# Gated linear recurrence: only the wanted blocks of each level, as 32x32 and 64x64 products over three banks, values two units later

## The chip, the cores and the metric

The kernel runs on one core of one Trainium2 chip. The metric is the time of an execution on the device, in microseconds; lower is better. Times come from several runs of the same program; a profile is one more execution, recorded by the hardware.

## The reference

Two transformer blocks run one after the other on 256 tokens of width 1024, each with two layers, all in float32. The change touches one mixer family of the second block, gated linear attention: four heads of GLA (keys of 32) and four heads of HGRN2 (keys of 64), values of 64.

```python
def chunked_gated_linear_attention(q, k, v, log_g):
    '''o_t = S_t^T q_t,  S_t = diag(exp(log_g_t)) S_{t-1} + k_t v_t^T, chunkwise.'''
    ...
        o_inter = jnp.einsum('bhik,bhkv->bhiv', q_ * jnp.exp(b_), state)
        rel = jnp.where(causal, b_[:, :, :, None, :] - b_[:, :, None, :, :], NEG)
        attn = jnp.einsum('bhik,bhjk,bhijk->bhij', q_, k_, jnp.exp(rel))
        o_intra = jnp.einsum('bhij,bhjv->bhiv', attn, v_)
```

Written without chunks: output token i is the sum over j <= i of (sum over the key's channels of q_i k_j exp(b_i - b_j)) v_j, where b is the running sum of the logarithm of the gate.

## The kernel before

**Levels.** The exponent b_i - b_j must not be split at a far border, or one factor overflows. The kernel therefore splits the pairs (i, j) by levels. At level l the tokens lie in blocks of 2n, n = 2^l, and a pair belongs to the level if j is in the first half of a block and i in the second. The border between the halves lies between them, so both factors are at most 1. `gaps` and `factors` build, for each level, one array GE that holds k times its decay in first halves and q times its decay in second halves. Levels 0 to 6 lie within 128 tokens; level 7 crosses from the first 128 tokens to the last 128; a product of plain k and q supplies the diagonal.

**Units.** There are 16 units in a layer: 8 heads (`FAM` has families 0, 1, 2; family 0 the GLA heads with 32 key channels, the others HGRN2 with 64) times two halves t of the tokens. Units 0 to 7 are GLA. For a unit TensorE forms eight products of 128x128 (L1706 for seven levels, L1708 for the diagonal) into PSUM banks 0 and 1, and for t = 1 the cross product of level 7 (L1711) into bank 2. Each product is a whole 128x128, of which the level wants only some blocks. VectorE multiplies the 1024 columns by a table of ones and zeros, `lvl_upper` (L1809, into `MASKED`), and adds the eight levels (L1811, into `AA`); ScalarE copies the cross product (L1748, into `ACR`). TensorE then multiplies by the values (L1685, and L1688 for the cross part) into bank 3.

**Order.** Every engine has an order written out by hand. `GLA_ORDER` lists the steps of the recurrence, `weave` puts after each of them one step of the other mixers (compressed attention, then four passes of softmax attention: NSA for t = 0 and 1, differential for t = 0 and 1). In step u TensorE issues the products of unit u, then the values of unit u-1, then its step of the others. An engine executes its instructions in that order, and waits for another engine by semaphores:

- TensorE's products of unit u wait for `gla_read` of unit u-1 (VectorE's mask has left banks 0 and 1), its values for `gla_A` and `gla_cross_out`.
- VectorE's mask waits for `gla_prod` of its unit. Its step of the other mixers stands behind its mask and sum: L1566 to L1574 (normalising the compressed key, read by TensorE's L1405), L1578 to L1587 (softmax of the compressed scores, read by L1419), L1067 to L1071 (scale, bias and maximum of a softmax), L1078 to L1081 (its sum and weights, read by L1029).
- TensorE's steps of the other mixers are L1399, L1405, L1412, L1419, L1424, and in a softmax pass L1022 (scores), L1029 (transposes) and L1038 (values); ScalarE's exponentials are L1047.
- POOL computes `gaps` and `factors` of families 1 and 2; for family 2 it waits for the products of unit 7.

In the setup POOL builds the level tables (`setup_pool`) into `lvl_upper`.

## Time and profile before

| | us |
|---|---|
| median of 3 runs | 2918.5 (2915.23 to 2920.84) |
| the profiled execution, its own time | 2915.66 |
| its span, first to last instruction | 2914.0 |
| TensorE busy (products) | 2657.3 (91%) |
| VectorE busy | 706.7 (24%) |
| ScalarE busy | 463.4 (16%) |
| POOL busy | 124.9 (4%) |

The two stretches with the recurrence are from 971 to 1113 us (layer 0 of the second block) and from 1657 to 1805 us (layer 1). Busy shares there differ from those of the whole: a share of the span says how long an engine had something under way, and not that it set the pace. A row of the time line gives the start, the time to the end of the last, the engine, the line, what is written and read, the shapes and the number of instructions merged in the row; in brackets stands how long the engine was idle before, and what ended that. A float32 product is two instructions, so 14 in a row are seven products. "32*128 32x128" is a weight block of 32 rows by 128 columns, and 128 moving columns on 32 rows. The clock in the tables (PEclk) is the share of 2.4 GHz that was granted: 0.50 is 1.2 GHz.

### The profile page before, as it was taken

The numbers are of one execution on the slowest core, as the hardware profiler recorded it, in microseconds if no ns is written. First come the engines' busy times: TensorE is split into PE (matmuls) and PEld (weight loads), VectorE is DVE, ScalarE is ACT, GpSimd is POOL, SyncE is SP. The second block draws the span as 40 slices with busy tenths as digits, with TensorE's granted clock in tenths as the row PEclk, the third lists the DMA queues.
The fourth block names the chain that finished last, engine by engine and source line by source line (L and its number), as shares of the span: only waits on it lengthen the run. The fifth ranks groups of instructions, "written<-read, shape, count | busy, mean of one in ns | idle before, by whom it ended". The sixth has DMA issues, their size and how long they took to land. (4 is left out here: it accounts for less than half of the span.)

```text
span 2914.0 us, 43737 instructions
## 1 busy us (share of the span) xinstructions
PE 2657.3 (91%) x19755; PEld 1489.0 (51%) x19755; DVE 706.7 (24%) x1244; ACT 463.4 (16%) x754; POOL 124.9 (4%) x320
## 2 busy tenths in 40 slices
PE   8899999999988776999979776799999999999997
PEld 7566558566534663444434475435445344353443
DVE  3434523434421653000011455200001000010002
ACT  1522311412212221001011321100000000000001
POOL 3011000010000110000000020000000000000000
PEclk9999999999999557999999755799999999999998
DMA  7321333312335101344434300399999999999990
GB/s 224 117 73 59 126 110 132 129 59 87 116 123 139 58 1 58 116 149 139 155 122 124 110 1 1 114 366 358 388 350 370 374 361 381 357 370 376 355 367 26
DMA packets 181230, 542.06 MB, mean 186 GB/s; under 512 B 26896, under 2 KB 38320, under 8 KB 181040
## 3 DMA queue, kind: packets, MB, share of 16 engines
q1 hardware_dynamic: 167744, 536.95, 51.1%
q10 hardware_dynamic: 12992, 1.22, 0.4%
q8 instruction: 158, 2.59, 0.3%
q0 software_dynamic: 304, 1.05, 0.1%
q14 instruction: 32, 0.26, 0.0%
HBM read 538.12 MB, written 1.05 MB: 185 GB/s over the span
## 5 line engine op out<-in xcount | busy, mean ns | idle before, releaser
L367 PE MATMUL psum<-ring,hT 128*128 128x512 f32 (+2 forms) x1856 | 783.0, 580 | 14.8 <-ACT area L606 13.2
L367 PEld LDWEIGHTS psum<-ring,hT 128*128 128x128 f32 x1856 | 346.0, 194 | 414.8 <-issue 393.5
L2106 PE MATMUL psum<-ring,area 128*32 128x448 f32 x4608 | 439.2, 539 | 2.6 <-ACT area L2208 2.0
L2106 PEld LDWEIGHTS psum<-ring,area 128*32 128x32 f32 x4608 | 150.0, 110 | 285.5 <-issue 282.0
L493 PE MATMUL psum<-hT,ring 128*128 128x256 f32 x768 | 166.5, 379 | 0.0
L493 PEld LDWEIGHTS psum<-hT,ring 128*128 128x128 f32 x768 | 145.8, 190 | 20.6 <-issue 1.0
L2125 PE MATMUL psum<-area 128*32 128x256 f32 x2688 | 149.8, 380 | 2.0 <-ACT area L2226 2.0
L2125 PE MATMUL psum<-ring,area 128*32 128x256 f32 x2688 | 151.5, 380 | 0.0
L2106 PE MATMUL psum<-area 128*32 128x448 f32 x1536 | 147.3, 539 | 0.0
L2125 PEld LDWEIGHTS psum<-area 128*32 128x32 f32 x2688 | 85.7, 110 | 60.2 <-ACT area L2226 3.9
L2259 DVE TENSOR_TENSOR area<-area,psum 128x1344 f32<-128x1344 f32 x16 | 24.9, 1554 | 372.1 <-PE psum L2106 372.1
L1706 PE MATMUL psum<-area 32*128 32x128 f32 (+1 forms) x448 | 103.2, 416 | 12.5 <-DVE area L1655 10.3
L2125 PEld LDWEIGHTS psum<-ring,area 128*32 128x32 f32 x2688 | 84.9, 110 | 57.0 <-issue 2.7
L1706 PEld LDWEIGHTS psum<-area 32*128 32x128 f32 (+1 forms) x448 | 94.2, 315 | 20.6 <-DVE area L1655 10.5
L1863 PE MATMUL psum<-ring,area 128*128 128x512 f32 x224 | 98.1, 601 | 1.2 <-ACT area L1874 1.2
L2106 PEld LDWEIGHTS psum<-area 128*32 128x32 f32 x1536 | 50.6, 110 | 93.8 <-issue 93.8
L2226 ACT ACTIVATE area<-psum 128x384 f32<-128x384 f32 x56 | 24.9, 488 | 408.5 <-PE psum L2121 408.5
L418 PE MATMUL psum<-ident,xn 128*128 128x128 f32 x132 | 30.1, 419 | 61.8 <-DVE xn L444 61.8
L1863 PEld LDWEIGHTS psum<-ring,area 128*128 128x128 f32 x224 | 43.1, 193 | 55.6 <-issue 54.2
L1029 PE MATMUL psum<-ident,area 128*128 128x128 f32 x120 | 23.5, 366 | 52.5 <-DVE area L1081 30.5
L2250 DVE TENSOR_TENSOR x<-x,psum 128x1024 f32<-128x1024 f32 x16 | 19.5, 1222 | 201.4 <-PE psum L2089 201.4
L2495 POOL DMA_DIRECT2D area<-in_p_dram x2 | 1.5, 758 | 1515.7 <-DVEq L214 1515.7
(453 smaller groups left out, 2426.8 us busy)
## 6 DMA issues: line engine op xcount, KB each, us to landing
ring<-in_w_in_dram SPq DMA_DIRECT2D x96, 1024.0 KB, 5.0
ring<-in_moe_w_gate_dram SPq DMA_DIRECT2D x96, 896.0 KB, 6.7
ring<-in_moe_w_up_dram SPq DMA_DIRECT2D x96, 896.0 KB, 7.8
area<-in_moe_w_down_dram SPq DMA_DIRECT2D x112, 512.0 KB, 7.5
ring<-in_moe_w_down_dram SPq DMA_DIRECT2D x112, 512.0 KB, 7.0
area<-in_moe_w_gate_dram SPq DMA_DIRECT2D x32, 896.0 KB, 6.7
area<-in_moe_w_up_dram SPq DMA_DIRECT2D x32, 896.0 KB, 8.3
ring<-in_w_out_dram SPq DMA_DIRECT2D x16, 1024.0 KB, 5.0
```

The costliest lines, as they stand in the source:

```text
L367: last = nc.tensor.matmul(acc(g)[:, t, 0:d["n"]], lhs(kk, t), w[:, k, :], start=kk == 0, stop=kk == d["nk"] - 1)
L418: last = nc.tensor.transpose(PS[0:m, bank0 + b // 2, (b % 2) * S + t * P:(b % 2) * S + (t + 1) * P], src, IDENT)
L493: last = nc.tensor.matmul(acc(g)[:, j // 2, (j % 2) * S:(j % 2) * S + S], half_view(n, (4, 512))[:, k % 4, j * P:(j + 1) * P], HT[:, k, :] ...
L1029: last = nc.tensor.transpose(PS[:, 4 + h // 2, ((h % 2) * T + j) * P:((h % 2) * T + j + 1) * P], SCORES[:, h, j * P:(j + 1) * P], IDENT)
L1706: nc.tensor.matmul(PS[:, l // 4, (l % 4) * P:(l % 4 + 1) * P], GE[f % 2][r, l, tok], GE[f % 2][r, l, tok], start=True, stop=True)
L1863: last = nc.tensor.matmul(PS[:, 2 * t + dh, :], HFT[:, 2 * i + k, t * P:(t + 1) * P], w[:, k, 512 * dh:512 * dh + 512], start=i + k == 0, ...
L2106: last = nc.tensor.matmul(PS[32 * j:32 * j + 32, 3 * p + b, 0:PIECE], XG[:, k, 32 * b:32 * b + 32], expert_slot(j0 + j // 2, GROUP * (j % ...
L2125: return nc.tensor.matmul(PS[32 * jj:32 * jj + 32, b, 0:256], HET[:, i // 4, b, 32 * (i % 4):32 * (i % 4) + 32], ring_cols(chunk_place(i) ...
L2226: nc.scalar.activation(HET[:, c], PS[:, 6 + c % 2, 0:BLOCKS * P].rearrange("p (b s) -> p b s", b=BLOCKS), ACT.Copy).then_inc(ms("HT"), 1)
L2250: nc.vector.tensor_tensor(X[:, t, :], X[:, t, :], banks(6, 2), ALU.add).then_inc(ms("added"), 1)
L2259: nc.vector.tensor_tensor(h, h, PS[:, 3 * p:3 * p + 3, 0:PIECE], ALU.mult).then_inc(ms("h"), 1)
L2495: pool.dma_start(PP, A["p_2"][L].rearrange("b (t p) c -> p (b t) c", p=P))\
```

## The change

Each level now forms only the blocks that it wants. Levels 0 to 4 and the diagonal have their pairs within 32 tokens: four blocks of 32x32 each, written to the partitions of their own tokens, so that six levels lie side by side in 192 columns. Level 5 is two blocks of 32x32, level 6 one of 64x64, level 7 stays a 128x128. Units go over banks 0, 1 and 2 in turn instead of sharing 0 and 1. VectorE masks and adds 192 columns instead of 1024. ScalarE copies the rest of each unit (levels 5, 6 and, for t = 1, 7: 96 or 224 columns) without a mask, after VectorE has read the bank. The values are five products and, for t = 1, a sixth, and follow two units later; three sets of `PARTS` hold a unit's factors. PSUM columns and parts that no product writes are set to zero once in a layer by VectorE. ScalarE's copy of the first eight outputs moves from unit 8 to unit 10.

```diff
-        MASKED = view(20656, 8 * P)
-        AA = [view(6456 + 128 * i, P) for i in range(2)]
-        ACR = [view(6712 + 128 * i, P) for i in range(2)]
+        MASKED = [view(20656 + 192 * i, 192) for i in range(2)]
+        PARTS = [view(a, 288) for a in (6456, 21040, 21328)]
...
             def out(u):
+                a = PARTS[u % 3]
                 pe.wait_ge(sem("gla_A"), 16 * L + u + 1)
+                pe.wait_ge(sem("gla_far"), 16 * L + u + 1)
...
-                last = nc.tensor.matmul(dst, AA[u % 2], U2[:, t, v0:v0 + HD], start=True, stop=t == 0)
+                for b in range(4):
+                    r = slice(32 * b, 32 * b + 32)
+                    nc.tensor.matmul(dst[r], a[r, 0:32], U2[r, t, v0:v0 + HD], start=True, stop=False)
+                last = nc.tensor.matmul(dst, a[:, 32:160], U2[:, t, v0:v0 + HD], start=False, stop=t == 0)
                 if t == 1:
-                    pe.wait_ge(sem("gla_cross_out"), 8 * L + u // 2 + 1)
-                    last = nc.tensor.matmul(dst, ACR[u // 2 % 2], U2[:, 0, v0:v0 + HD], start=False, stop=True)
+                    last = nc.tensor.matmul(dst, a[:, 160:288], U2[:, 0, v0:v0 + HD], start=False, stop=True)
...
-                if u:
-                    pe.wait_ge(sem("gla_read"), 16 * L + u)
-                for l in range(LEVELS):
-                    nc.tensor.matmul(PS[:, l // 4, (l % 4) * P:(l % 4 + 1) * P], GE[f % 2][r, l, tok],
-                                     GE[f % 2][r, l, tok], start=True, stop=True)
-                last = nc.tensor.matmul(PS[:, 1, 3 * P:4 * P], TT[r, FAM[f][1], tok], TT[r, FAM[f][0], tok],
-                                        start=True, stop=True)
+                if u >= 3:
+                    pe.wait_ge(sem("gla_far"), 16 * L + u - 2)
+                ps = PS[:, u % 3]
+                for b in range(4):
+                    blk, c = slice(t * P + 32 * b, t * P + 32 * b + 32), slice(32 * b, 32 * b + 32)
+                    for l in range(5):
+                        nc.tensor.matmul(ps[c, 32 * l:32 * l + 32], GE[f % 2][r, l, blk], GE[f % 2][r, l, blk],
+                                         start=True, stop=True)
+                    nc.tensor.matmul(ps[c, 160:192], TT[r, FAM[f][1], blk], TT[r, FAM[f][0], blk], start=True, stop=True)
+                    if b % 2 == 0:
+                        up = slice(t * P + 32 * b + 32, t * P + 32 * b + 64)
+                        nc.tensor.matmul(ps[c, 192 + 32 * b:224 + 32 * b], GE[f % 2][r, 5, blk], GE[f % 2][r, 5, up], start=True, stop=True)
+                last = nc.tensor.matmul(ps[0:64, 224:288], GE[f % 2][r, 6, t * P:t * P + 64],
+                                        GE[f % 2][r, 6, t * P + 64:t * P + 128], start=True, stop=True)
...
-                if u:
-                    out(u - 1)
+                if u >= 2:
+                    out(u - 2)
                 yield
+            out(14)
             out(15)
...
+                    s.eng.wait_ge(sem("gla_read"), 16 * L + u + 1)
+                    if u >= 3:
+                        s.eng.wait_ge(sem("gla_out"), 16 * L + u - 2)
+                    n = 96 + 128 * UNITS[u][2]
+                    s.after(nc.scalar.activation(PARTS[u % 3][:, 64:64 + n], PS[:, u % 3, 192:192 + n], ACT.Copy)
+                            .then_inc(sem("gla_far"), 1), "gla_far")
...
+            s.do(nc.vector.memset(PS[:, 0:3, 192:288], 0.0))
+            for a in PARTS:
+                s.do(nc.vector.memset(a[:, 32:64], 0.0))
...
-                    s.after(nc.vector.tensor_tensor(MASKED, banks(0, 2), mt_t[:, :], ALU.mult)
+                    s.after(nc.vector.tensor_tensor(MASKED[u % 2], PS[:, u % 3, 0:192], near_t[:, :], ALU.mult)
                             .then_inc(sem("gla_read"), 1), "gla_read")
-                    s.after(nc.vector.tensor_reduce(AA[u % 2], MASKED.rearrange("p (l c) -> p c l", l=8), AX.X, ALU.add).then_inc(sem("gla_A"), 1), "gla_A")
+                    if u >= 3:
+                        s.eng.wait_ge(sem("gla_out"), 16 * L + u - 2)
+                    s.after(nc.vector.tensor_reduce(PARTS[u % 3][:, 0:32], MASKED[u % 2].rearrange("p (l c) -> p c l", l=6),
+                                                    AX.X, ALU.add).then_inc(sem("gla_A"), 1), "gla_A")
...
-            s.do(g.tensor_copy(MT[:, LEVELS, :], IDENT))
+            for b in range(4):
+                r = slice(32 * b, 32 * b + 32)
+                s.do(g.tensor_copy(NEAR[r, 0:5, :], MT[r, 0:5, r]))
+                s.do(g.tensor_copy(NEAR[r, 5, :], IDENT[r, r]))
```

In the changed kernel the products are lines 1712 (levels 0 to 4), 1714 (diagonal), 1717 (level 5), 1718 (level 6) and 1721 (level 7), the values 1688 (four of 32x64), 1689 and 1691, VectorE's mask and sum 1821 and 1825, ScalarE's copy 1763.

TensorE's order from the transposed compressed key (L1405) to the compressed scores (L1412), with unit 3 between them, before:

```order
L1405 MATMUL psum<-ident,area 128x128
L1706 MATMUL psum<-area 128x128 x7
L1708 MATMUL psum<-area 128x128
L1711 MATMUL psum<-area 128x128
L1685 MATMUL psum<-area 128x64
L1412 MATMUL psum<-area 128x32 x8
```

and after (here a row's number counts products, each of two passes):

```order
L1405 MATMUL psum<-ident,area 128x128
L1712 MATMUL psum<-area 32x32 x5
L1714 MATMUL psum<-area 32x32
L1717 MATMUL psum<-area 32x32
...
L1718 MATMUL psum<-area 64x64
L1721 MATMUL psum<-area 128x128
L1688 MATMUL psum<-area 32x64 x4
L1689 MATMUL psum<-area 128x64
L1691 MATMUL psum<-area 128x64
L1412 MATMUL psum<-area 128x32 x8
```

Left out are the same rows for the other three blocks of 32 tokens (L1717 for every second one). Nine products of unit 3 have become 28, and the values in that step are those of unit 1 instead of unit 2.

VectorE and ScalarE, the step of unit 2, with what each instruction waits for; before, VectorE:

```order
L1809 TENSOR_TENSOR area<-psum,lvl_upper 128x1024 [waits gla_out,gla_prod,cmp_by_vector]
L1811 TENSOR_REDUCE area<-area 128x128 [waits gla_read]
L1569 RECIPROCAL small<-small 128x1 [waits cmp_by_scalar,gla_A]
L1570 SCALAR_TENSOR_TENSOR area<-psum,small,param_rows 128x64 [waits dve_steps]
L1571 COPY area<-area 128x64 [waits dve_steps]
```

after, VectorE:

```order
L1821 TENSOR_TENSOR area<-psum,lvl_upper 128x192 [waits gla_prod,cmp_by_vector]
L1825 TENSOR_REDUCE area<-area 128x32 [waits gla_read]
L1569 RECIPROCAL small<-small 128x1 [waits cmp_by_scalar,gla_A]
L1570 SCALAR_TENSOR_TENSOR area<-psum,small,param_rows 128x64 [waits dve_steps]
L1571 COPY area<-area 128x64 [waits dve_steps]
```

and ScalarE after, where before there was a copy (L1748) only for units with t = 1:

```order
L1763 ACTIVATE area<-psum 128x224 [waits gla_read,cmp_by_scalar]
L1467 ACT_TABLE_LOAD [waits cmp_by_vector]
L1467 ACTIVATE small<-small 128x1 [waits gla_far]
L1763 ACTIVATE area<-psum 128x96 [waits gla_read,cmp_by_scalar]
L1470 ACTIVATE area<-psum 128x128 [waits cmp_by_tensor,gla_far]
```

Nothing has changed its place between the steps; the unit's work on VectorE is narrower, and ScalarE has a copy in every unit, which waits for VectorE's mask.

## Rows read from the trace of the kernel before

**Rows 1.** Stretches: us, busy us and count of each engine, clock, DMA.

```profile
972.00:1113.00 141.00, 105.20 (x508) 94.68 (x508) 80.74 (x79) 30.96 (x91) 21.52 (x48) 0.55 0.00 1
1657.00:1805.00 148.00, 115.11 (x507) 104.07 (x507) 81.13 (x81) 30.72 (x91) 21.69 (x48) 0.50 0.00 0
1062.00:1076.00 14.00, 11.61 (x105) 10.81 (x104) 10.72 (x11) 1.24 (x2) 5.18 (x12) 0.99 0.00 1
663.00:669.00 6.00, 6.00 (x119) 5.94 (x117) 1.47 (x6) 0.77 (x2) 0.53 (x2) 0.50 0.02 6
```

**Rows 2.** Time line of TensorE's products, layer 1, units 2 to 4.

```profile
1668.38 3.32 PE L1706 MATMUL psum<-area 32*128 32x128 f32 x14 [0.86 <-DVE area L1809]
...
1676.18 0.48 PE L1405 MATMUL psum<-ident,area 128*128 128x128 f32 x1 [3.01 <-DVE area L1571]
1676.58 3.35 PE L1706 MATMUL psum<-area 32*128 32x128 f32 x14
1679.73 0.63 PE L1708 MATMUL psum<-area 32*128 32x128 f32 x2
1680.16 0.63 PE L1711 MATMUL psum<-area 32*128 32x128 f32 x2
1680.72 0.69 PE L1685 MATMUL psum<-area 128*128 128x64 f32 x2
...
1692.07 0.69 PE L1419 MATMUL psum<-ident,area 128*128 128x128 f32 x2 [4.04 <-DVE area L1587]
```

**Rows 3.** The same, units 10 to 15.

```profile
1751.03 7.04 PE L1038 MATMUL psum<-area 128*128 128x64 f32 x32
...
1762.75 1.26 PE L1022 MATMUL psum<-area 32*128 32x128 f32 x16
...
1774.11 1.12 PE L1029 MATMUL psum<-ident,area 128*128 128x128 f32 x4 [5.35 <-DVE area L1081]
...
1801.88 1.97 PE L1029 MATMUL psum<-ident,area 128*128 128x128 f32 x8 [8.64 <-DVE area L1081]
```

**Rows 4.** Time line of VectorE, layer 1, units 2 to 4.

```profile
1672.22 1.23 DVE L1809 TENSOR_TENSOR area<-psum,lvl_upper 128x1024 f32<-128x1024 f32 x1 [1.84 <-PE psum L1708]
1673.48 1.90 DVE L1811 TENSOR_REDUCE area<-area 128x128 f32<-128x1024 f32 x1
...
1675.93 0.19 DVE L1571 COPY area<-area 128x64 f32<-128x64 f32 x1
...
1684.81 0.42 DVE L1580 TENSOR_REDUCE small<-area 128x8 f32<-128x256 f32 x1
...
1688.34 1.94 DVE L1811 TENSOR_REDUCE area<-area 128x128 f32<-128x1024 f32 x1
1690.31 0.42 DVE L1584 TENSOR_REDUCE small<-area 128x8 f32<-128x256 f32 x1
```

**Rows 5.** The same, unit 11.

```profile
1763.56 1.93 DVE L1811 TENSOR_REDUCE area<-area 128x128 f32<-128x1024 f32 x1
1765.52 1.22 DVE L1067 SCALAR_TENSOR_TENSOR area<-psum,causal_bias 128x1024 f32<-128x1024 f32 x1
```

**Rows 6.** Time line of TensorE, first block, 64x64 weights at the lower clock.

```profile
666.50 1.04 PE L803 MATMUL psum<-area 64*64 64x32 f32 x16
667.36 1.04 PE L799 MATMUL psum<-area 64*64 64x32 f32 x16
```

**Rows 7.** The page's costliest groups: us busy, ns of one.

```profile
L2125 PE MATMUL psum<-area 128*32 128x256 f32 x2688 | 149.8, 380 | 2.0 <-ACT area L2226 2.0
```

**Rows 8.** Time line of TensorE, layer 1, scores of the first softmax pass.

```profile
1704.01 3.09 PE L1022 MATMUL psum<-area 64*128 64x128 f32 x16
1707.03 3.35 PE L1706 MATMUL psum<-area 32*128 32x128 f32 x14
```

**Rows 9.** Groups of instructions by shape, 1657 to 1806 us, ScalarE.

```profile
L1748 ACT ACTIVATE area<-psum 128x128 f32<-128x128 f32 x8 | 2.2, 277 | 35.8 <-PE psum L1711 35.7
```

**Rows 10.** Time line of TensorE, layer 0, unit 0.

```profile
971.51 3.35 PE L1706 MATMUL psum<-area 32*128 32x128 f32 x14 [5.17 <-DVE area L1655]
```

More of the change, by code:

```diff
@@ L126, in blocks_kernel @@
         IDENT2 = eye_t[:, :]
-        mt_t = sb("lvl_upper", (LEVELS + 1) * P)
-        MT = mt_t[:, :].rearrange("p (l c) -> p l c", l=LEVELS + 1)
+        near_t = sb("lvl_upper_32", 6 * 32)
+        NEAR = near_t[:, :].rearrange("p (l c) -> p l c", l=6)
         cb_t = sb("causal_bias", T * S)
@@ L1702, in gla_pe @@
                     pe.wait_ge(sem("hg_GE"), 2 * L + f)
-                if u:
-                    pe.wait_ge(sem("gla_read"), 16 * L + u)
-                for l in range(LEVELS):
-                    nc.tensor.matmul(PS[:, l // 4, (l % 4) * P:(l % 4 + 1) * P], GE[f % 2][r, l, tok],
-                                     GE[f % 2][r, l, tok], start=True, stop=True)
-                last = nc.tensor.matmul(PS[:, 1, 3 * P:4 * P], TT[r, FAM[f][1], tok], TT[r, FAM[f][0], tok],
-                                        start=True, stop=True)
+                if u >= 3:
[12 more added lines that the diff above has]
+                                        GE[f % 2][r, 6, t * P + 64:t * P + 128], start=True, stop=True)
                 if t == 1:
-                    last = nc.tensor.matmul(PS[:, 2, (u // 2 % 2) * P:(u // 2 % 2 + 1) * P], GE[f % 2][r, 7, 0:P],
-                                            GE[f % 2][r, 7, P:S], start=True, stop=True)
+                    last = nc.tensor.matmul(ps[:, 288:416], GE[f % 2][r, 7, 0:P], GE[f % 2][r, 7, P:S],
+                                            start=True, stop=True)
                 last.then_inc(sem("gla_prod"), 1)
-                if u:
-                    out(u - 1)
+                if u >= 2:
+                    out(u - 2)
                 yield
+            out(14)
             out(15)
@@ L1743, in gla_act @@
                 elif kind == "unit":
-                    if UNITS[u][2] == 1:
-                        s.eng.wait_ge(sem("gla_prod"), 16 * L + u + 1)
-                        if u >= 4:
-                            s.eng.wait_ge(sem("gla_out"), 16 * L + u - 3)
-                        s.after(nc.scalar.activation(ACR[u // 2 % 2], PS[:, 2, (u // 2 % 2) * P:(u // 2 % 2 + 1) * P],
-                                                     ACT.Copy).then_inc(sem("gla_cross_out"), 1), "gla_cross_out")
-                    if u == 8:
+                    if u == 10:
                         s.eng.wait_ge(sem("gla_out"), 16 * L + 8)
@@ L2366, in setup_pool @@
             wide_low = view(1024, P)
+            MT = view(1152, LEVELS * P).rearrange("p (l c) -> p l c", l=LEVELS)
             for l in range(LEVELS):
```

4 lines of the change are left out of this document (1 added, 3 removed).

## The prediction

> **What bounds the kernel now.** I began with the granted clock and the busy shares of the two stretches in which the gated recurrence runs [rows 1]. One stands in each layer of the second block, 141 us long in layer 0 and 148 us in layer 1. TensorE is busy 105 of 141 and 115 of 148 us, VectorE 81 in both, and no weights arrive. The clock is at its lower level (1.2 GHz) in all of layer 1's stretch; in layer 0's, 14 us ran near 2.4 GHz, and that stretch is about 7 us shorter. The stage is a relay between TensorE, VectorE and ScalarE with TensorE the runner on most legs, so its own order of time comes next [rows 2, 3], then VectorE's [rows 4, 5]. The reader is to see two sorts of TensorE time: work back to back, and waits that end with VectorE. Four such waits have VectorE's work on a unit in front of what TensorE wants.
>
> - The products of unit 2 wait 0.86 us until unit 1 has been read from the same two banks [rows 2].
> - L1405 waits 3.01 us for the copy L1571, which stands behind unit 2's mask and sum (1.23 + 1.90 us) [rows 2, 4].
> - L1419 waits 4.04 us for a chain whose first link, L1584, starts the moment unit 4's sum (1.94 us) ends [rows 2, 4].
> - L1029 waits 5.35 us in the differential attention. There L1067 starts as unit 11's sum ends, although its scores (L1022, 1.26 us from 1762.75) are there at about 1764.1 [rows 3, 5].
>
> The wait of 8.64 us [rows 3] is a softmax of 2048 columns on VectorE and ScalarE; the change takes at most 0.1 us from it.
>
> **VectorE's work on a unit.** L1067 takes 1.22 us for 1024 columns, L1580 0.42 for 256, so a column costs 1.04 ns and an instruction 0.15 us besides [rows 4, 5]. The mask on 192 columns then takes 0.36. The strided sum is dearer, 1.93 us for 1024 columns [rows 5]; its share for 192 is 0.36, and with an instruction's fixed part counted again 0.5; I take 0.45. A unit goes from 3.15 us (with gaps) to 0.85: 2.3 us less, 32 times. That is 74 us of VectorE, and nearly all of it hidden. What shows, for layer 1: 0.9 (now three banks) + 2.3 (L1405) + 2.3 (L1419, whose exponentials are ready by then) + 1.4 (L1029: 1765.5 less 1764.1) + 0.1 = **7.0 us**. For layer 0 I take the same; its waits have the same causes.
>
> **TensorE's work on a unit.** Each product is two passes, and a pass is what a row counts. A pass with weights of 128 columns and 128 moving ones costs 0.43/2 = 0.215 us (L1708 to L1711), and a run of 14 takes 3.15, which is 0.14 more; from the last pass of a run to the next run in another shape of the array goes 0.56 instead of 0.43 [rows 2]. So a change of shape costs 0.14 + 0.13 = 0.27 us. L1038, with half as many moving columns (64), still costs 7.04/32 = 0.22 a pass [rows 3]: a pass costs the longer of its weight load and its product, not their sum. At the same low clock 64x64 weights run in 0.86/16 = 0.054 a pass, two tiles of the array at a time, hence 0.107 a pass in one tile [rows 1, 6]. No row has 32 columns on both sides. Half of 0.107 is 0.054; that is what the two sizes at hand (128: 0.215, 64: 0.107) extrapolate to, and it is my value. The bounds are 0.107 (no gain below 64 columns) and 0.014 (0.054 in four column tiles fully at once, as L2125 runs: 149.8/2688 = 0.056 us a pass where its 256 columns alone take 0.21 at the high clock [rows 7]).
>
> How far do the four column tiles of a unit overlap? L2125 changes tile every second pass. The new unit stays in one tile for 14, 12, 14 and 12 passes. The nearest row is L1022 with two runs of eight in two tiles: 3.02 us to the next start, less 0.27, is 12.8 passes of 0.215 for 16 [rows 8]. So a run starts some three passes before the one ahead of it ends. Three changes of tile save nine of 52 passes: 43 x 0.054 = 2.3 us.
>
> Per unit, in passes (TensorE's order is shown above):
> - removed: 16 passes, 3.44 us, and 0.27 for the shape. The cross product of every second unit (0.43) stays.
> - added: the 32x32 run 2.3 + 0.27; the 64x64 product 2 x 0.107 + 0.27 = 0.48; the four 32x64 value products, each in its own tile, 2 x 0.107 and a little, 0.27, + 0.27 = 0.54; in every second unit 0.27 more, because the 128x128 cross product is now a shape of its own.
> - even unit: 2.57 + 0.48 + 0.54 = 3.59 against 3.71, so 0.12 less; odd unit: 0.15 more. The mean is nothing, though the number of products has trebled.
>
> Some 12 of 16 units lie on the path (those ahead of the softmax waits don't), so +0.2 us at most. At the end of the stage values of two units instead of one are due between L1029 and L1038: +0.5. **A layer changes by -7.0 + 0.7 = -6.3 us, both together by -12.6.**
>
> **Hidden edits.** ScalarE's copy is 0.28 us for 128 columns [rows 9]; now it copies 96 or 224 of every unit, behind VectorE's mask. Its readers come two units later, so it costs nothing; if ScalarE were late by a whole step, TensorE would wait at L1688. The four memsets (0.7 us at 0.42 for 256 columns and 0.1 to 0.15 for the small ones) delay the compression's input, and TensorE stands idle for 5.17 us before unit 0, until its factors are there [rows 10]. POOL's eight small copies for one large stand in the setup, 0.3 us each or less; the first products that need these constants are far behind. Queues of DMA are not touched.
>
> **The sum.** The profiled execution took 2915.66 us (span 2914.0), the median of the runs is 2918.5. Against its own time the sum gives 2903 if layer 0 keeps its stretch at the high clock and, with 7 us more, 2910 if not. Against the median, which I take because that stretch need not come in each run, it is 2918.5 - 12.6 = 2905.9, so **2906 us**. A measurement of this kernel can tell about 0.2%, 5.8 us, from no change.
>
> **Rivals.**
> 1. *Small passes in one row group do not overlap* (slower). All 32x32 products of a unit read the same 32 or 64 partitions. If a pass there costs load plus product, 0.107, the run takes 43 to 52 x 0.107 = 4.6 to 5.6 us instead of 2.3, on 12 units of each layer: +27 to +40, less 6: 2960 to 2986. The price decides from 0.066 a pass on: there 43 x 0.012 us on 12 units is 6.2 us a layer, and gain and loss balance. For it: no row shows 32 columns. Against it: L1706 lies in one row group too, and there the load hides [rows 2, 3]. Chance 0.11; a price between would give 2925 to 2950. The Trainium skill (TensorE: Matmul & The Clock Gate, Part 3, "What overlaps and what doesn't") states just this: a weight load overlaps with products in flight only when the row group differs. By that rule L1706 would take 0.43 a pass, and the trace has 0.215, so I hold to the row.
> 2. *The long runs are serial*: a run waits for the last pass of the one before, or a 32-column pass costs 0.066. 52 x 0.054 = 2.8 us, +0.5 x 12 = +6 a layer: the gain on VectorE is paid back, 2917. For it: only two tiles were seen in L1022. Chance 0.17.
> 3. *The column tiles overlap nearly fully*, as in L2125: the run takes about 1.2 us, another 1.1 x 12 = 13 us a layer: 2880. Against it are runs of 14 instead of 2. Chance 0.10.
> 4. *The sum is right, but layer 0 loses its high clock*: smaller products, more changes of shape. It had 141 us where layer 1 had 148 [rows 1]: 2915.66 - 12.6 + 7 = 2910. Chance 0.12.
> 5. *The change does not take the waits away*, because ScalarE's copy, which waits on VectorE's mask, becomes what TensorE waits for. It would show as L1712 waiting on L1763. Its time is that of rival 2; its chance is in that one.
>
> The forecast has 0.50. The range **2890 to 2922** holds it, rivals 2 and 4 and the dearer half of 3. Faster by over 0.2% means below 2912.7: forecast 0.50, rival 3 0.10, and two thirds of rival 4, 0.08: 0.68. Within 0.2%: rival 2 and the rest of 4: 0.21. Slower: 0.11.
>
> **What would show it.** In the profile after: L1712's run from its first start to L1718's in 2.2 to 2.7 us at the low clock; L1821 near 0.36 and L1825 near 0.45 us; L1405 waiting under 1 us and L1419 under 2.3; L1029 after the last scores still 8 us or so; L1712 never waiting for L1763. Layer 1's stretch from L1712's first start to L1038's last run should be 141 to 142 us instead of 148. Wrong would be a run of 4 us or more (rival 1), 2.9 (2) or 1.2 (3), or a wait of TensorE on L1763.

## The result and the profile after

The changed kernel takes **2891.1 us** (median of 4, 2889.8 to 2892.2), the kernel before, run beside it, 2919.1 (2915.2 to 2920.8): a ratio of **0.9906, interval 0.9889 to 0.9923**. That is 28 us faster, where 13 were forecast. The direction held, and the range by 1.1 us; the size did not. The profiled execution took 2891.88 us, its span is 2890.2; it is 23.8 us shorter than that of the kernel before. The times of one kernel go with its mean granted clock: the runs of the kernel before made here go from 2923.3 us at 0.912 to 2907.3 at 0.920 (one of 6954 us left out). So of the 28 us a few can be clock.

The two stretches, in the view of [rows 1]:

```profile
972.00:1112.00 140.00, 111.71 (x1259) 96.51 (x1259) 44.92 (x83) 34.12 (x100) 21.63 (x49) 0.50 0.01 1
1648.00:1787.00 139.00, 111.70 (x1259) 96.49 (x1259) 44.18 (x80) 33.96 (x99) 21.62 (x48) 0.50 0.00 1
```

A *pass* is one of the two instructions of a float32 product. VectorE has gone from 81 to 44 us; TensorE is about as busy as it was (112 us in both, 105 and 115 before), with 1259 passes instead of 508. The clock (0.50) is low in both layers now; the 14 us near 2.4 GHz in layer 0 are gone. From here on a *stage* is the time from the first product of unit 0 to the start of the last L1038, read from the time line: 141.3 us in layer 0 and 147.9 in layer 1 before, 135.3 in both after.

TensorE's time line of layer 1, which answers to [rows 2, 3]:

```profile
1660.74 0.47 PE L1405 MATMUL psum<-ident,area 128*128 128x128 f32 x1 [0.79 <-DVE area L1571]
1661.14 0.74 PE L1712 MATMUL psum<-area 32*32 32x32 f32 x10
...
1661.70 0.26 PE L1712 MATMUL psum<-area 32*32 32x32 f32 x1
...
1662.72 0.26 PE L1712 MATMUL psum<-area 32*32 32x32 f32 x1
...
1663.49 0.47 PE L1718 MATMUL psum<-area 32*64 32x64 f32 x2
1663.89 0.79 PE L1721 MATMUL psum<-area 32*128 32x128 f32 x2
1664.61 0.44 PE L1688 MATMUL psum<-area 32*32 32x64 f32 x8
1664.98 0.69 PE L1689 MATMUL psum<-area 128*128 128x64 f32 x2
...
1674.24 0.69 PE L1419 MATMUL psum<-ident,area 128*128 128x128 f32 x2 [2.55 <-DVE area L1587]
...
1752.32 1.12 PE L1029 MATMUL psum<-ident,area 128*128 128x128 f32 x4 [5.02 <-DVE area L1081]
...
1779.13 1.97 PE L1029 MATMUL psum<-ident,area 128*128 128x128 f32 x8 [8.45 <-DVE area L1081]
```

From start to start: the 52 passes of 32x32 take 2.35 us, the 64x64 product 0.40, the four small value products 0.37. A *column tile* is the part of TensorE's array that holds 32 columns of weights; a unit's run of 32x32 products goes through four of them. Passes of one tile start every 0.0533 us. The second tile's first pass (1661.70) comes 0.56 us after the run's start, though the first tile has 14 passes, 0.75 us, and the fourth tile's (1662.72) after 1.58 us, though 40 passes, 2.13 us, lie before it. A tile so starts 3.5 passes before the one ahead of it ends. The waits at L1405 and L1419 are 0.79 and 2.55 us instead of 3.01 and 4.04. No product waits for ScalarE's copy. VectorE and ScalarE, unit 2, which answer to [rows 4]:

```profile
1659.07 0.36 DVE L1821 TENSOR_TENSOR area<-psum,lvl_upper 128x192 f32<-128x192 f32 x1 [1.69 <-PE psum L1718]
1659.46 0.48 DVE L1825 TENSOR_REDUCE area<-area 128x32 f32<-128x192 f32 x1
...
1660.49 0.20 DVE L1571 COPY area<-area 128x64 f32<-128x64 f32 x1
```

```profile
1659.52 0.25 ACT L1763 ACTIVATE area<-psum 128x96 f32<-128x96 f32 x1 [0.56 <-DVE area L1821]
```

### The profile page after: what moved, and what is told of

The parts are those of the page before. It is cut to its first block, busy times and chain, and to the rows that moved or that the text cites. A ratio compares the mean times of both kernels' runs of the same rounds, so it can differ in the third digit from the quotient of the medians.

```text
span 2890.2 us, 46780 instructions
## 1 busy us (share of the span) xinstructions
PE 2650.3 (92%) x21227; PEld 1475.8 (51%) x21227; DVE 633.8 (22%) x1252; ACT 468.9 (16%) x770; POOL 127.9 (4%) x327
## 4 chain that ended last, share of the span: by engine, by line
PE 54%; DVE 3%; ACT 2%; issue 0%; DVEq 0%; ACTq 0%; PEldq 0%
PE psum L2121 20%; PE psum L367 12%; PE psum L2140 10%; PE psum L1878 3%; PE psum L2096 1%; PE psum L2104 1%; PE psum L1261 1%; PE psum L418 1%; PE psum L1712 1%; PE psum L2136 1%; PE psum L1038 1%; ACT area L1047 0%; PE psum L1022 0%; PE psum L1029 0%; DVE area L1067 0%
## 5 line engine op out<-in xcount | busy, mean ns | idle before, releaser
L367 PE MATMUL psum<-ring,hT 128*128 128x512 f32 (+2 forms) x1856 | 780.5, 578 | 14.8 <-ACT area L606 13.2
L367 PEld LDWEIGHTS psum<-ring,hT 128*128 128x128 f32 x1856 | 345.2, 193 | 413.2 <-issue 391.8
L2140 PEld LDWEIGHTS psum<-area 128*32 128x32 f32 x2688 | 85.7, 110 | 60.2 <-ACT area L2241 3.9
L1712 PE MATMUL psum<-area 32*32 32x32 f32 (+1 forms) x1280 | 74.0, 239 | 9.0 <-DVE area L1654 9.0
L1712 PEld LDWEIGHTS psum<-area 32*32 32x32 f32 (+1 forms) x1280 | 69.7, 149 | 17.3 <-DVE area L1654 9.2
L1029 PE MATMUL psum<-ident,area 128*128 128x128 f32 x120 | 23.5, 366 | 48.7 <-DVE area L1081 26.9
L2233 ACT ACTIVATE area<-psum 128x1344 f32<-128x1344 f32 x16 | 20.5, 1291 | 269.7 <-PE psum L2121 269.7
```

The source lines that it names most:

```text
L367: last = nc.tensor.matmul(acc(g)[:, t, 0:d["n"]], lhs(kk, t), w[:, k, :], start=kk == 0, stop=kk == d["nk"] - 1)
L1712: nc.tensor.matmul(ps[c, 32 * l:32 * l + 32], GE[f % 2][r, l, blk], GE[f % 2][r, l, blk], start=True, stop=True)
L2140: return nc.tensor.matmul(PS[32 * jj:32 * jj + 32, b, 0:256], HET[:, i // 4, b, 32 * (i % 4):32 * (i % 4) + 32], ring_cols(chunk_place(i) ...
```

## The experiments

All runs are of this program on one core; ratios are to runs of the kernel before on the same chip. Columns "1405", "1029b" are the time from the first product of unit 0 to L1405 and to the L1029 of the second pass, in layer 1; up to there every kernel is at the low clock. "High" is the length of a stretch at high clock within a stage. All in us. Stages, waits and clocks are read from one profiled execution of each kernel.

| kernel | median | ratio (interval) | 1405 | 1029b | stage 0 (high) | stage 1 (high) |
|---|---|---|---|---|---|---|
| before | 2919.1 | 1 | 19.1 | 85.7 | 141.3 (13.6) | 147.9 (0) |
| after | 2891.1 | 0.991 (0.989-0.992) | 12.7 | 75.2 | 135.3 (0) | 135.3 (0) |
| e1 alternate | 2863.8 | 0.982 (0.980-0.984) | 8.9 | 64.1 | 119.8 (0) | 119.5 (3.4) |
| e2 smalls last | 2891.8 | 0.992 (0.990-0.994) | 12.7 | 75.6 | 134.2 (3.4) | 135.9 (0) |
| e3 before, narrow VectorE | 2888.9 | 0.991 (0.989-0.993) | 15.9 | 80.4 | 133.0 (13.6) | 133.2 (13.7) |
| e4 wider VectorE | 2899.4 | 0.995 (0.993-0.996) | 14.4 | 78.2 | 137.5 (3.4) | 137.8 (3.4) |
| e5 VectorE as before | 2897.7 | 0.993 (0.991-0.995) | 15.6 | 80.0 | 139.3 (3.4) | 139.3 (3.4) |
| e6 alternate, far too | 2849.1 | 0.977 (0.975-0.978) | 8.3 | 60.6 | 114.8 (3.4) | 114.8 (3.4) |
| e7 level 6 twice | 2895.0 | 0.992 (0.990-0.994) | 13.4 | 76.9 | 137.3 (3.4) | 136.7 (3.4) |
| e8 values one behind | 2883.7 | 0.989 (0.987-0.990) | 13.7 | 75.7 | 128.2 (13.6) | 134.8 (0) |
| e9 level 6 inside | 2900.7 | 0.993 (0.991-0.995) | 13.7 | 77.6 | 138.9 (0) | 138.2 (3.4) |
| e10 e1, VectorE as before | 2869.5 | 0.984 (0.982-0.985) | 12.7 | 69.2 | 123.9 (3.4) | 124.0 (3.4) |
| e11 e6, values one behind | 2845.7 | 0.974 (0.972-0.977) | 8.3 | 60.3 | 110.8 (3.4) | 110.6 (3.4) |
| e12 e6, other order | 2839.3 | 0.973 (0.971-0.975) | 8.3 | 60.5 | 107.1 (3.4) | 107.1 (3.4) |
| e13 before, narrow sum | 2896.1 | 0.994 (0.992-0.996) | 17.7 | 83.1 | 136.5 (13.7) | 136.9 (13.6) |
| e14 e5 in one bank | 2907.3 | 0.997 (0.996-0.998) | 17.0 | 81.3 | 141.3 (3.4) | 141.6 (3.4) |
| e15 e11, order 2 | 2838.8 | 0.974 (0.972-0.976) | 8.3 | 63.3 | 108.8 (3.4) | 108.3 (3.5) |
| e16 e6, order 2 | 2833.3 | 0.972 (0.971-0.974) | 8.2 | 58.3 | 106.2 (0) | 106.2 (0) |

### VectorE's part: e3, e13, e4, e5

e3 and e13 edit the kernel before, e4 and e5 the changed one:

```diff
 # e3 (e13 keeps the mask product whole); both leave columns 192 to 1023 out of the result
-nc.vector.tensor_tensor(MASKED, banks(0, 2), mt_t[:, :], ALU.mult)
+nc.vector.tensor_tensor(MASKED[:, 0:192], PS[:, 0, 0:192], mt_t[:, 0:192], ALU.mult)
-nc.vector.tensor_reduce(AA[u % 2], MASKED.rearrange("p (l c) -> p c l", l=8), ...)
+nc.vector.tensor_reduce(AA[u % 2][:, 0:32], MASKED[:, 0:192].rearrange("p (l c) -> p c l", l=6), ...)
 # e5, ahead of the mask; a second one with 146 columns ahead of the sum (e4: 58 and 96)
+s.do(nc.vector.tensor_reduce(view(6744, 82), bc(CB[:, 0, 0:82].unsqueeze(2), [P, 82, 8]), AX.X, ALU.add))
```

> The kernel before, with the mask product and the sum over levels cut from 1024 to 192 columns of 128 partitions; the other columns are left out of the result, TensorE's work is the same as before. Theory A (my prediction's VectorE part: 7.0 us of TensorE's waits a layer go, the rest of the 12.7 us that the change gained a layer is TensorE's own): a stage of about 141 us instead of 147.9 in layer 1, the kernel about 2905 us. Rival B (VectorE's shorter work is the whole gain, the small products cost what the large ones did): 135 us, about 2892 us. Rival C (TensorE was bound by itself and the waits move elsewhere): 147 us, 2918 us.

> The kernel before, with only the sum over levels cut from 1024 to 192 columns (1.92 to about 0.48 us; the other columns are left out of the result), the mask product still on 1024 columns. In the run with both cut, the stage of layer 1 shrank by 14.7 us, of which about 8 us came with a 13.7 us stretch of high clock that the kernel before has only in layer 0; anchor by anchor, where both were at the low clock, it was 5.4 us up to the first L1029. Theory A (VectorE's part at equal clock is 7 us for 2.31 us a unit, so that the sum alone, 1.44 us a unit, is 3 to 5 us): L1405 about 2 us and L1419 about 3.5 us earlier than before (17 and 31.5 us after the start), the stage 143 to 145 us if it stays at the low clock; the kernel about 2909 us, or 2902 us with a high stretch in layer 1. Rival B (VectorE's shorter work really is worth 14.7 us a layer without the clock): 139 us at the low clock.

> The changed kernel with two idle sums on VectorE in each unit (464 and 768 elements of a constant), so that the mask product ends about 1.23 us and the unit's sum about 3.15 us after the start, as in the kernel before; TensorE's work is that of the change. Theory A (a hand count of the stage with TensorE's durations from the changed kernel and VectorE's from the one before): the stage grows by about 5 us to 140.5 us, the kernel by 10 to about 2901 us. Rival B (two units of slack and three banks hide VectorE whatever it takes, the gain is all TensorE's own): 135.3 us, 2891 us. Rival C (VectorE was the whole gain): 148 us, 2916 us or more.

> The changed kernel with two larger idle sums on VectorE (656 and 1168 elements): in the last run the two took 0.64 and 0.95 us, so a unit cost VectorE 2.43 us and not the 3.15 us of the kernel before, and the stage of layer 1 grew from 135.3 to 137.8 us. With 0.88 and 1.44 us it should be as in the kernel before. Theory A (what VectorE costs a unit is partly hidden by three banks and two units of slack, the rest shows at L1405 and L1419): 139 to 141 us a stage, the kernel 2900 to 2903 us. Rival B (the added 0.72 us a unit is all on the path of 16 units): 149 us, 2920 us. Rival C (what is hidden stays hidden): 138 us, 2899 us.

e3 took 2888.9 us, what its rival B names: VectorE's columns alone seem to be worth the whole change. The granted clock forbids that reading. Windows of e3 and, at the same work, of the kernel before, layer 1:

```profile
1728.00:1742.00 14.00, 11.83 (x108) 11.07 (x107) 6.84 (x13) 3.68 (x11) 5.73 (x13) 0.99 0.00 1
```

```profile
1741.00:1755.00 14.00, 12.19 (x55) 11.63 (x56) 3.38 (x3) 5.55 (x10) 7.51 (x16) 0.50 0.00 0
```

e3 does twice the passes there. The same L1038 x32 as in [rows 3], 7.04 us, takes 3.74 in e3, and a unit's 14 passes 1.82 instead of 3.35:

```profile
1730.29 3.74 PE L1038 MATMUL psum<-area 128*128 128x64 f32 x32
1733.95 1.82 PE L1706 MATMUL psum<-area 64*128 64x128 f32 x14
...
1746.01 1.12 PE L1029 MATMUL psum<-ident,area 128*128 128x128 f32 x4 [6.18 <-DVE area L1081]
```

Two comparisons are free of the clock. Up to 1029b in layer 1, all at the low clock, e3 is 5.4 us earlier, e13 2.7. In layer 0 before, e3 and e13 have the same high stretch: stages 141.3, 136.5 and 133.0. Of both cuts' 8.2 us 3.2 are there by L1405, 2.1 come at L1419 and 2.1 at L1029 of the third pass; the other 0.8 come because the high stretch begins earlier against the work. Without these VectorE is worth **7.4 us** a layer in the old order, and the sum alone 4.4. The prediction's 7.0 stands. e13 gave less than A's 2 and 3.5 us (1.4 by L1405, 2.7 by L1419); its median of 2896 lies below the 2902 that A gave for a high stretch in layer 1, and no run shows why.

e4 undershot its own aim (2.43 us a unit instead of 3.15), and its stage grew by 2.5 us instead of 5. e5 comes near the aim (0.84 + 0.36 + 1.37 + 0.48 = 3.05 us); its groups of VectorE in layer 1:

```profile
L1826 DVE TENSOR_REDUCE area<-causal_bias 128x146 f32<-128x1168 f32 x16 | 21.9, 1370 | 0.6
L1821 DVE TENSOR_REDUCE area<-causal_bias 128x82 f32<-128x656 f32 x16 | 13.4, 836 | 36.0 <-PE psum L1721 18.1 <-PE psum L1718 17.8
```

With VectorE as slow as before, the new kernel has a stage of 139.3 us: theory A by the stage, though the median, 2897.7, lies 2 us below A's and nearer to C's. That is 4.1 us more than after, and 5.4 at equal clock (5.0 in layer 0), since 1.3 us come back between 1029b and the scores of the third pass (17.8 us against 19.1), where e5 has 3.4 us of high clock. The rest of the 12.7 us, 7.3, is TensorE's, the banks' and the lag's. 7.4 for VectorE in the old order and 7.3 for the rest are 2.0 us more than both together bring: either hides a part of the other.

### The banks: e14

```diff
-                if u >= 3:
-                    pe.wait_ge(sem("gla_far"), 16 * L + u - 2)
-                ps = PS[:, u % 3]
+                if u >= 1:
+                    pe.wait_ge(sem("gla_far"), 16 * L + u)
+                ps = PS[:, 0]
```

> The changed kernel with VectorE's work as before (stage 139.3 us, 2898 us) and with all units in bank 0 instead of taking turns over three, so that the products of a unit wait for the mask and the copy of the unit before, much as in the kernel before. Theory A (three banks hide 1 to 3 us a layer of VectorE's 3.15 us a unit, at units with no other step between): the stage 140.5 to 142.5 us, 2900 to 2905 us, and the mask of 1.2 us plus ScalarE's copy of 0.36 us shown ahead of L1712. Rival B (the values of two units ago and the other mixers' step fill that time): 139.3 us, 2898 us. Rival C (the waits show in every unit, 1 us or more): 150 us or more.

The stage grew by 2.0 and 2.3 us (A: 1 to 3), and the wait stands where A put it:

```profile
1662.51 0.71 PE L1712 MATMUL psum<-area 32*32 32x32 f32 x10 [1.93 <-ACT area L1763]
```

So the banks hide about the 2.0 us by which the two parts above overlap. e14 is the kernel nearest to the one before in everything but TensorE's products and the lag: 141.6 us, or 142.9 if the high clock gave it the same 1.3 us as e5, against 147.9. Those 5.0 us are what the prediction had as +0.7.

### The price of shapes: e7, e9, e2

```diff
 # e7: the level 6 product once more, into the same place
+                nc.tensor.matmul(ps[0:64, 224:288], GE[f % 2][r, 6, t * P:t * P + 64],
+                                 GE[f % 2][r, 6, t * P + 64:t * P + 128], start=True, stop=True)
 # e9: the same product under "if b == 2" inside the loop over b, instead of behind it
 # e2: in out(), the 128-row products first (start=True), then the four 32-row ones
```

> The changed kernel with the 64-column product of level 6 (L1718, 0.40 us from start to next start) issued twice in each unit, into the same place. This parts the price of a product into its passes and what comes once for the change of shape. Theory A (two passes of 0.107 us, and 0.19 us once): the pair takes 0.61 us, a stage 2.5 to 3 us more, the kernel about 2896 us. Rival B (each product costs its 0.40 us): the pair 0.80 us, a stage 5 us more, 2901 us.

> The changed kernel with the 64x64 product of level 6 in the middle of the 32x32 run (after the second of four column tiles) instead of behind it; the same products, but the 32x32 shape is entered twice in a unit. Theory A (entering the shape of 32 columns costs about 0.06 us, and 3 of 13 passes no longer overlap the tile before, 0.16 us): 0.2 us a unit, stage 137.5 to 138.5 us instead of 135.3, the kernel about 2896 us. Rival B (each change of shape costs 0.27 us, the price of my prediction, plus the overlap): 0.43 us a unit, stage 140 to 142 us, 2903 us. Rival C (shapes don't matter at all): 0.0 to 0.1 us a unit, 2891 to 2893 us.

> The changed kernel, with the four 32-row value products of a unit issued after its 128-row ones, directly ahead of the next unit's 32x32 run; same products. Even units then have three changes of shape instead of four, odd units three instead of five. Theory A (what is paid beside the passes is the change of shape, dearer for wider weights: about 0.12 us for one to 32 columns and 0.28 for one round through 128): 0.1 us less in even units, 0.3 in odd ones, a stage of about 133 us instead of 135.3, the kernel about 2886 us. Rival B (the price hangs on the products, not on their order): 135.3 us, 2891 us.

e7, time line, unit 2 of layer 1: two more passes put 0.21 us more between L1718 and L1688 (0.62 instead of 0.40), and L1405 comes 0.64 us later for three units. The stages grew by 2.0 and 1.5 us, where A said 2.5 to 3, but each has 3.4 us at the high clock that the changed kernel lacks. Counted in steps of 0.21 us, layer 0 shows 8 units on the path up to 1029b and 3 after the second L1038; the one between falls into the high clock. That bears out the 12 of the prediction:

```profile
1660.74 0.47 PE L1718 MATMUL psum<-area 32*64 32x64 f32 x2
1661.01 0.42 PE L1720 MATMUL psum<-area 32*64 32x64 f32 x2
1661.36 0.44 PE L1688 MATMUL psum<-area 32*32 32x64 f32 x8
```

So a pass of 64x64 is 0.107, as forecast, and what comes once is **0.19 us**, not 0.27. For the 32x32 run it is less: 52 passes are 2.77 us, the three changes of tile save 0.55, and the run takes 2.35, so **0.13**. (The expectation for e9 reckoned with 43 passes, nine saved, and so came to 0.06.) e9 splits that run; its unit 2:

```profile
1663.17 0.74 PE L1715 MATMUL psum<-area 32*32 32x32 f32 x10
...
1664.50 0.47 PE L1711 MATMUL psum<-area 32*64 32x64 f32 x2
1664.90 0.74 PE L1715 MATMUL psum<-area 32*32 32x32 f32 x10
...
1665.91 0.33 PE L1688 MATMUL psum<-area 32*32 32x64 f32 x4
...
1666.28 0.69 PE L1689 MATMUL psum<-area 128*128 128x64 f32 x2
```

The first half takes 1.33 us. In the units without values behind the run, and in the odd ones, where the cross product follows, the second half takes 1.33 us too: 0.31 more for both, of which 0.18 is the lost overlap of one change of tile and 0.13 the second entry. Both halves give the same 0.13 (26 passes are 1.39 us, less 0.18). In the even units nothing is lost: up to L1689 unit 2 takes 3.11 us, against 3.12 in the changed kernel. The small value products, also with 32 columns of weights, stand right behind the run there and begin before it ends. Theory A's 0.2 us a unit is too little for the odd units; its stage (137.5 to 138.5) is nearly met by 138.2 and 138.9, while the median, 2900.7, lies between A and B. e2 shows that the count of changes is no price list either. Its theory A, that one or two changes less would save 0.1 to 0.3 us a unit, fell, and rival B (135.3 us, 2891) held: the values of an even step ahead of L1022 take 0.37 + 0.62 us in the changed kernel and 0.62 + 0.37 in e2, those of an odd one 1.41 in both.

### How the column tiles overlap: e1, e6, e10

```diff
-                for b in range(4):
-                    blk, c = ...
-                    for l in range(5):
+                for l in range(7):
+                    for b in range(0, 4, 2 if l == 6 else 1):
+                        blk, c = ...
...
 # e6 in addition: level 6 as two, level 7 as four products with 32 columns of weights
+                for b in range(2):
+                    last = nc.tensor.matmul(ps[32 * b:32 * b + 32, 224:288],
+                                            GE[f % 2][r, 6, t * P + 32 * b:t * P + 32 * b + 32],
+                                            GE[f % 2][r, 6, t * P + 64:t * P + 128], start=True, stop=True)
```

> The changed kernel, with the small products of a unit issued level by level, so that the four column tiles take turns, instead of tile by tile; same products, same count. Theory A (passes of one column tile follow each other at 0.053 us, passes of different column tiles overlap, as the next tile's run already starts some 3 passes before the end of the last): the run of 52 passes falls from 2.35 us to 1.0 to 1.2 us at the low clock, a layer's stage from 135.3 to about 122 us, the kernel from 2891 to about 2865 us. Rival B (the pass has one price of 0.053 us whichever tile it is in, since one queue feeds all tiles): run 2.35 us, 2891 us. Rival C (taking turns costs a change of tile each time, 0.02 us or more): run 3.4 us, over 2903 us.

> The alternating kernel (stage 119.5 us, kernel 2864 us) with level 6 as two and the cross product of level 7 as four products with 32 columns of weights, so that these tiles too take turns; the results are the same. Theory A (a tile of 32 columns needs 0.053 us for 32 moving columns, tiles side by side are free): level 6 falls from 0.40 to about 0.25 us, level 6 with the cross product from 1.12 to about 0.65 us, 0.3 us a unit less; on the path in the third to half of the units that wait for nothing, so 2 to 4 us a layer, the kernel 2856 to 2860 us. Rival B (the alternating kernel now waits for VectorE and ScalarE at L1405, L1419 and L1029, what TensorE saves turns into longer waits): 119 to 120 us, 2863 us.

> The alternating kernel of the first runs (stage 119.5 us, 2864 us) with the idle sums on VectorE that give its unit the 3.15 us of the kernel before. In the changed kernel these cost 4.1 us a layer (135.3 to 139.3). Theory A (with a run of 0.9 us instead of 2.35 a unit costs TensorE about 2 to 3.4 us, less than VectorE's 3.15, so VectorE now sets the pace of many units): the stage grows by 8 to 14 us to 128 to 134 us, the kernel to 2882 to 2894 us, most of what alternating gained is gone. Rival B (the cost of VectorE is the same 4.1 us as with the long run): 123.6 us, 2872 us.

e1, time line, unit 3 of layer 1 at the low clock:

```profile
1643.00 0.76 PE L1713 MATMUL psum<-area 32*32 32x32 f32 x40
1643.56 0.31 PE L1716 MATMUL psum<-area 32*32 32x32 f32 x8
1643.66 0.30 PE L1719 MATMUL psum<-area 32*32 32x32 f32 x4
1643.90 0.47 PE L1720 MATMUL psum<-area 32*64 32x64 f32 x2
```

The same 52 passes take 0.90 us instead of 2.35, 40 of them 0.56: 0.014 each, near 0.0533 / 4. The run (0.90 us) and the stages (119.5 and 119.8) are shorter than even theory A said, the median of 2864 is what it said: 27 us less than the changed kernel. Here order alone decides how much of the array works at a time. In e6 levels 6 and 7 take turns over such tiles too:

```profile
1668.03 0.42 PE L1725 MATMUL psum<-area 64*32 64x128 f32 x2
...
1668.13 0.71 PE L1725 MATMUL psum<-area 64*32 64x128 f32 x6
1668.77 0.43 PE L1688 MATMUL psum<-area 32*32 32x64 f32 x8
```

L1713 started at 1667.24, so all products of an odd unit, now 64 passes, take 1.53 us, where the changed kernel needs 3.47 and e1 2.02. Their six far products take 0.63 us instead of the 1.12 of two whole ones. A stage lost 4.7 us more, beyond A's 2 to 4. e10's theory A fell: with the 32x32 run at 0.90 us instead of 2.35, the old VectorE work costs 4.5 us a layer, hardly more than the 4.1 of e5 (rival B). It is all there by L1419 (25.7 us after the start instead of 21.0); from L1419 to the end the two take 98.3 and 98.5 us.

### What is left: e8, e11, e12, e15, e16

```diff
 # e8 (on the changed kernel), e11 (on e6)
-                if u >= 2:
-                    out(u - 2)
+                if u >= 1:
+                    out(u - 1)
 # e12, for PE, DVE and ACT: steps of the other mixers done after each step of the recurrence
-evenly(GLA_STEPS, MIXER_STEPS)
+[1, 2, 3, 4, 5, 6, 7, 8, 9, 9, 10, 12, 12, 15, 15, 15, 18, 18, 21, 21, 21, 22, 23]
 # e15, e16: ... 12, 12, 14, 15, 15, 15, 18, 18, 21, 21, 22, 23
```

In e8, e11, e15 and e16 ScalarE's copy of the first eight outputs stands at unit 9.

> The changed kernel with the value products one unit behind instead of two. Theory A (with short VectorE work the inputs of a unit's values are there 1.3 us after its products, and the next unit's run of 2.35 us hides that): the stage stays within 0.5 us of 135.1 us, or 0.9 us less since one unit less is left at its end, the kernel 2890 to 2892 us. Rival B (two units of slack are needed, where VectorE is busy with the selection): a wait of 1 to 2 us at the value products in five or more units, a stage of 140 us or more, 2901 us.

> The kernel with all far products in 32-column tiles that take turns (stage 114.8 us, 2849 us), with the values one unit behind instead of two. In the changed kernel that took 0.5 us off the stage at the same clock. Theory A (a unit's products now take only 1.3 to 1.9 us, while mask, sum and copy take 0.36 + 0.48 and 0.36 us behind each other, so values one unit behind come about when their inputs do): within 1 us of 114.8 us, 2847 to 2851 us. Rival B (the values now wait for VectorE in most units, 0.3 us or more each): 118 us or more, 2855 us.

> The kernel with all far products in 32-column tiles that take turns (stage 114.8 us, 2849 us), with the steps of the other mixers set between the units by another list: two or three units stand between the scores (L1022) and the transposes (L1029) of each softmax pass, where TensorE waits 2.7, 9.1, 7 and 11 us a layer, and two ahead of L1419. Theory A (these waits are ScalarE's and VectorE's chain of the pass, which runs on while TensorE does units): 6 to 12 us a layer of waits are filled, stage 103 to 109 us, the kernel 2825 to 2838 us. Rival B (VectorE's masks and sums of the added units now stand ahead of the softmax's own steps, and the chain ends later by as much): 114 us, 2849 us or more.

> The kernel with another list of steps (stage 107.1 us, 2839 us), in which the values of unit 8 waited 8.14 us for ScalarE's copy of the first eight outputs, behind the exponentials of the second softmax pass. Now the values come one unit behind, and the scores of that pass come after unit 9, so that the copy stands ahead of the exponentials. Theory A (that wait was the step of the chain that had no work beside it): 4 to 7 us less a layer, stage 100 to 103 us, the kernel 2826 to 2833 us. Rival B (the chain of the softmax pass is what takes its 15 us from L1022 to L1029, and the wait only moves to L1029): 106 to 107 us, 2838 us.

> The kernel of the last run (stage 108.3 us, 2839 us; TensorE's value products waited 3.3, 7.4, 2.5 and 5.5 us for ScalarE's copies, L1767, which stand behind the exponentials of each softmax pass), with the values two units behind again and ScalarE's copy of the first eight outputs at unit 9. The copies that the values of a gap need are then done before its exponentials. Theory A (the waits were the order on ScalarE, since a copy takes 0.25 or 0.36 us): no wait over 1 us on L1767 or L1762, what was waited there goes partly into the waits at L1029; 3 to 7 us less a layer than 107.1 us, the kernel 2825 to 2833 us. Rival B (from L1022 to L1029 the chain of a softmax pass takes its time, 14.8 us in the second pass, and TensorE's work in that gap is all covered already): stage 105 to 107 us, 2835 to 2839 us.

e8: at the low clock (layer 1) the second unit of lag costs 0.5 us a layer: it brings 1.0 us by L1405 and takes 1.0 at the end of the stage and 0.5 on the way. The median fell by 7.4 us; the profile has a high stretch of 13.6 us in layer 0 that the changed kernel lacks, worth about as much. e11 gained 4 us a layer where A said within 1. Of that 2.1 us is the wait of unit 8's values for ScalarE's copy in e6, which is gone; the rest was not taken apart.

e12's stage of 107.1 us is theory A's; the moved units fill the waits, and meet a new one, on the copy L1762. In e15 it only changes its name, and with 108.3 us theory A fell:

```profile
1683.68 0.44 PE L1689 MATMUL psum<-area 32*32 32x64 f32 x8 [8.14 <-ACT mix L1762]
```

```profile
1686.41 0.44 PE L1689 MATMUL psum<-area 32*32 32x64 f32 x8 [7.40 <-ACT area L1767]
```

e16 takes both away, and only 1 us of stage follows. Its second pass:

```profile
1658.52 5.65 PE L1022 MATMUL psum<-area 64*128 64x256 f32 x16
...
1673.28 3.68 PE L1029 MATMUL psum<-ident,area 128*128 128x128 f32 x16 [4.10 <-ACT area L1047]
```

From L1022 to L1029 it takes 14.76 us, the same as in the kernel before (14.77): the chain of the pass, with three units' work in it. By the stage that is rival B; the median, 2833.3, is at the edge of A. That the softmax of the other mixers now sets the stage is what this pass suggests; no run tests it. e16, **2833 us**, has the lowest median, 0.972 of the kernel before (0.971 to 0.974), an interval that overlaps those of e12 and e15.

## Why the prediction was off

- **VectorE, 7.0 us a layer: right.** 7.4 at equal clock in the old order, and nearly part by part (e3): 3.2 by L1405, where 0.9 + 2.3 were forecast, 2.1 at L1419 (2.3) and 2.1 at L1029 of the third pass (1.4). L1821 takes 0.36 us (0.36 forecast), L1825 0.48 (0.45). L1419 was forecast to wait under 2.3 us and waits 2.55.
- **A pass of 32x32 at 0.054 us, a run starting three passes before the end of the last: right, the second in part by luck.** 0.0533 from start to start, and 3.5 passes instead of three. But the three were read from L1022 [rows 8], whose weights are 64 rows by 128 columns: its two tiles are halves of the rows, and the new ones quarters of the columns. No row showed that the two overlap alike. Rival 1, that load and product add up within one row group, did not come: with it the run would be over 4.6 us. The rule of the Trainium skill behind it (TensorE: Matmul & The Clock Gate, "What overlaps and what doesn't") disagrees with this trace: by it a pass of 32x32 in the row group of the one before would take 0.107.
- **The step that failed: a change of shape costs 0.27 us.** It was read at weights of 128 columns [rows 2], where it holds (the cross product takes 0.72 us, 0.43 + 0.29), and charged alike for 32 and 64. Measured: 0.13 for the 32x32 run, 0.19 for the 64x64 product, 0.16 (0.37 less 2 x 0.107) for the small value products. A unit is shorter by 0.22 + 0.08 + 0.17 = 0.47 us than forecast: an even one took 3.12 us against 3.71, not 3.59; an odd one 3.84 against 4.14, not 4.29. Of the 0.47, the price of a change of shape is 0.33, the closer overlap of the tiles 0.08, the "little" added to the value products 0.06. Times the 12 units on the path (e7) the 0.47 is 5.6 us a layer, and -6.3 - 5.6 is -11.9 of the measured -12.7 at the low clock. So TensorE's own part was not +0.7 but -4.9; e14 measures -5.0. The sentence "The mean is nothing" hid it, and VectorE's part was left to look like the whole gain. The +0.5 for the values at the end was right in sum (e8).
- **Hidden edits: right.** TensorE never waits for L1763, and stands idle for 4.20 us ahead of unit 0 in layer 1 instead of 5.16, still until its factors are there (VectorE's L1654).
- **Rival 3 (column tiles overlap nearly fully) did not come, but was near.** Its time of 2880 and more stood behind the order of the two loops: e1.
- **Rival 4 came true in the profile, on top of all that:** layer 0 lost its stretch at high clock and gained 6.0 us instead of 12.7. Its reason (smaller products, more changes of shape) is not borne out: e8 has the same products, and the stretch, in layer 0; its median is 2883.7. That the result lies within the range is luck: with those 6.7 us it would have been about 2884, below 2890.
- **Outside the stages** the profiled spans differ by another 5.1 us of 23.8, though the code there is the same: 4.4 between the stages (539.9 us against 544.3), 2.1 behind them, less 1.4 ahead. In the kernels run here that middle part lies anywhere from 539.9 to 544.5 us. The traces show where the 4.4 comes from. The same 128 passes of L367 behind layer 0 take 58.21 us before (from 1172.20) and 55.17 after (from 1167.13): the clock is at 0.50 around their start, in three windows of 3.5 us before and in one after. That is 3.0 us. A second such place, at 1376 us, has a clock of 0.54 before and 1.00 after and gives 1.7, which a low clock of the changed kernel takes back near the end of the part; 1.0 is the shorter wait ahead of unit 0, 0.4 the last steps of layer 0. So most of it is the clock, and not the work of the recurrence. What decides when the clock falls stays open, and with it how much of the 28.0 is the change's own.

## What to carry to other kernels

When a large matmul is cut into small blocks, read the cost of a change of shape at the size of weights that the new code uses, or bound it from both sides; charged at the large size and thrice a unit it hid 4 us of a gain of 12.7 a layer. Put products of different column tiles next to each other: the same passes took 2.35 or 0.90 us by the order of two loops. And compare a shortened chain by anchors at equal clock before believing a total, since e3's total credited VectorE with the whole gain.

## What was not expected of the hardware

- Column tiles work side by side when consecutive products differ in tile: 0.0533 us a pass in one tile, 0.014 with four in turn, at 1.2 GHz. Between long runs only 3.5 passes overlap. Products of 32 columns of weights with 64 and 128 moving columns overlap too (e6: 0.63 us for six).
- A short product costs less behind one of the same weight width: in e9's even units the value products overlap the end of the 32x32 run, and splitting that run costs nothing there.
- A stretch of 13.6 us at high clock stood in the second pass or was missing, with the same code there: before has it in layer 0 and not in layer 1; e3 and e13, which differ from it on VectorE alone, have it in both. It begins 3.3 to 5.0 us after the start of L1029 x16 of that pass, which a wait of 9.1 us precedes; so does the place where it is missing. It is worth 6.7 us of a stage (147.93 less 141.26). What decides was not tried.
